# Sums of squares of the attention keys: from column sums and diagonals to a matrix of ones

## What is computed

```python
def mla(c_q, c_kv, k_rope, cq_g, w_uq, ckv_g, w_uk, w_uv, qn_g, kn_g, cos, sin):
    q = (rms_norm(c_q, cq_g) @ w_uq).reshape(b_, t_, MLA_HEADS, QK_HEAD)
    ckv = rms_norm(c_kv, ckv_g)
    k_nope = (ckv @ w_uk).reshape(b_, t_, MLA_HEADS, QK_NOPE)
    v = (ckv @ w_uv).reshape(b_, t_, MLA_HEADS, V_HEAD)
    k_r = jnp.broadcast_to(k_rope[:, :, None, :], (b_, t_, MLA_HEADS, QK_ROPE))
    k = jnp.concatenate([k_nope, k_r], axis=-1)
    q = rms_norm(q, qn_g)
    k = rms_norm(k, kn_g)
    ...
    o = causal_block_attention(q, k, v)
```

## Time and profile before

| | us |
|---|---|
| median of three runs | 1754.62 |
| lowest and highest | 1753.00 and 1754.93 |
| the profiled execution | 1751.97 |
| its span, first to last instruction | 1750.2 |
| PE busy in it | 1734.3 (99%) |
| DVE, ACT, POOL busy | 813.8, 467.3, 1183.7 |
| mean granted TensorE clock | 0.999 of 2.4 GHz |

### The profile page before, as it was taken

The page is one execution under the profiler, slowest core; times in us unless marked ns, Lnnn a source line. Parts: engine busy times, 40 slices in busy tenths (PEclk is TensorE's granted clock), DMA queues, the critical chain, the costliest instruction groups (busy, mean ns, idle before and its releaser), DMA issues.

```text
span 1750.2 us, 32871 instructions
## 1 busy us (share of the span) xinstructions
PE 1734.3 (99%) x12264; PEld 1626.1 (93%) x12264; DVE 813.8 (46%) x1373; ACT 467.3 (27%) x843; POOL 1183.7 (68%) x1365
## 2 busy tenths in 40 slices
PE   7999999999999999999999999999999999999999
PEld 7999999999999999999999999989998888888887
DVE  7755546455555452212347546464555554422221
ACT  4423223242323331101134232332323233311110
POOL 7754746374798777777766647473847988777773
PEclk9999999999999999999999999999999999999999
DMA  4321212122322223222431312222222222422233
GB/s 158 123 96 54 90 59 84 65 74 70 109 84 84 84 96 130 88 96 85 161 112 64 105 56 74 72 84 68 72 77 104 85 93 86 145 88 92 96 121 110
DMA packets 47489, 161.60 MB, mean 92 GB/s; under 512 B 5408, under 2 KB 6816, under 8 KB 47136
## 3 DMA queue, kind: packets, MB, share of 16 engines
q1 hardware_dynamic: 41328, 146.56, 24.6%
q10 hardware_dynamic: 6112, 14.39, 2.2%
HBM read 152.27 MB, written 10.81 MB: 93 GB/s over the span
## 4 chain that ended last, share of the span: by engine, by line
PE 96%; DVE 2%; ACT 1%; issue 0%; ACTq 0%; DVEq 0%
PE slots L508 83%; PE slots L566 4%; PE slots L599 3%; PE slots L542 2%; PE slots L660 2%; PE slots L584 1%; PE slots L551 1%; DVE h_lo L1099 1%; DVE branch_lo L1111 1%; DVE h_tile L1175 0%; PE slots L701 0%; DVE spare L1120 0%; PE slots L569 0%; ACT cq_hi L849 0%; DVE early L1165 0%
## 5 line engine op out<-in xcount | busy, mean ns | idle before, releaser
L420 POOL TENSOR_TENSOR w_lo<-w_raw,w_hi 128x256 fp32r<-128x256 f32 x1004 | 828.4, 855 | 20.9
L415 POOL TENSOR_SCALAR w_hi<-w_raw 128x1024 fp32r<-128x1024 f32 x251 | 284.0, 1131 | 388.1 <-PE slots L508 380.7
L508 PE MATMUL slots<-h_hi,w_hi 128*128 128x264 f32 (+1 forms) x2112 | 522.8, 311 | 0.6
L508 PE MATMUL slots<-h_lo,w_hi 128*128 128x264 f32 (+1 forms) x2112 | 515.9, 308 | 0.0
L508 PE MATMUL slots<-h_hi,w_lo 128*128 128x264 f32 (+1 forms) x2112 | 515.1, 308 | 0.0
L508 PEld LDWEIGHTS slots<-h_hi,w_hi 128*128 128x128 f32 x2112 | 342.7, 188 | 22.9 <-issue 3.9
L508 PEld LDWEIGHTS slots<-h_hi,w_lo 128*128 128x128 f32 x2112 | 342.0, 188 | 19.1
L508 PEld LDWEIGHTS slots<-h_lo,w_hi 128*128 128x128 f32 x2112 | 342.0, 188 | 17.6
L508 PE MATMUL slots<-branch_hi,w_hi 128*128 128x264 f32 (+1 forms) x576 | 144.0, 313 | 9.6 <-DVE branch_lo L1111 8.9
L508 PE MATMUL slots<-branch_lo,w_hi 128*128 128x264 f32 (+1 forms) x576 | 142.8, 311 | 0.0
L508 PE MATMUL slots<-branch_hi,w_lo 128*128 128x264 f32 (+1 forms) x576 | 142.4, 311 | 0.0
(11 more groups left out here) (243 smaller groups left out, 2825.0 us busy)
## 6 DMA issues: line engine op xcount, KB each, us to landing
w_raw<-w_units SPq DMA_DIRECT2D x251, 512.0 KB, 3.2
stream<-sc_acc ACTq DMA_DIRECT2D x16, 264.0 KB, 3.0
sc_back<-stream SPq DMA_DIRECT2D x2, 2112.0 KB, 8.7
x_old<-stream SPq DMA_DIRECT2D x16, 264.0 KB, 4.4
stream<-residual_or_merged ACTq DMA_DIRECT2D x16, 264.0 KB, 2.5
ab_raw<-w_units SPq DMA_DIRECT2D x8, 512.0 KB, 4.6
residual_or_merged<-xt ACTq DMA_DIRECT2D x4, 528.0 KB, 7.6
stream<-xt ACTq DMA_DIRECT2D x1, 2112.0 KB, 10.3
```

The source lines that it names most:

```text
L415: pool.tensor_scalar(hi, raw, 1.0, 1.0, ALU.mult, ALU.mult).then_inc(sem("hi_part"), 1)
L420: op = pool.tensor_tensor(lo[:, cols], raw[:, cols], hi[:, cols].bitcast(F32), ALU.subtract)
L508: mm = pe.matmul(out[:, a_, 0:t1 - t0], w(k), x(k)[:, t0:t1], start=(n == 0), stop=(n == 3 * ks - 1))
```

## The change

The keys' sums of squares are made on all partitions at once. The new `spread_sum` multiplies a 128x128 matrix of ones (the weights) by the squares (what moves, 264 columns at a time), so that PSUM holds the sum for every token on every partition. DVE adds the rope share, which now is a 128x528 tile `kr_sum` in SBUF, ACT takes the root of 528 columns in place, DVE the reciprocal of 528 columns in place, and keys and rope part are multiplied by that tile, which lies in SBUF (`early4`, `early5`). Column sums, diagonals and spreading matmuls for the keys are gone. For kr, `stat_kr` becomes `sum_kr`, copied to SBUF by DVE and multiplied twice by the spread norm of the input.

Several things move with it. The two sums stand between `vb` and `qn0` on PE. `rot` stands behind four pieces of fill; one piece, `stat_q` and nine pieces follow (before: `rot`, two pieces, `stat_q`, twelve pieces; three of them stand inside `stat_q` in both). Of the slots, `qn0` goes to 2, `qn1` to 3, `qr` to 0, `rot` to 2, `stat_q` to 3, and the fills with `av0` and `av1` exchange 0 and 1. In CQ, kr comes before q1, and `rot` behind `stat_q`; DVE's work on q1 stands behind the last column tile of the input's norm.

```diff
-FILLS = (2, 12, 5, 5, 6, 6, 7, 2, 6, 6, 7, 7, 6)
+FILLS = (4, 1, 9, 5, 5, 6, 6, 7, 2, 6, 6, 7, 7, 6)
-           ("stat_kr", 2, "cq_mm"), ("rot", 3, "cq_mm"), ("stat_q", 1, "cq_mm")],
+           ("sum_kr", 2, "cq_mm"), ("stat_q", 1, "cq_mm"), ("rot", 3, "cq_mm")],
-            ("qn0", 0, "att_mm"), ("stat_k", 1, "att_mm"), ("qn1", 2, "unit_used"), ("qr", 3, "att_mm"),
-            ("spread_k0", 0, "att_mm"), ("spread_k1", 1, "att_mm"), ("rot", 3, "att_mm"), ("stat_q", 2, "att_mm"),
...
-            ("g1", 0, "unit_used"), ("b1", 1, "unit_used"), ("ga1", 0, "unit_used"), ("av1", 1, "att_mm")],
+            ("sum_k0", 0, "att_mm"), ("sum_k1", 1, "att_mm"), ("qn0", 2, "att_mm"), ("qn1", 3, "unit_used"),
+            ("qr", 0, "att_mm"), ("rot", 2, "att_mm"), ("stat_q", 3, "att_mm"),
...
+            ("g1", 1, "unit_used"), ("b1", 0, "unit_used"), ("ga1", 1, "unit_used"), ("av1", 0, "att_mm")],
...
+            def spread_sum(out, squares):
+                for a_ in range(2):
+                    mm = pe.matmul(out[:, a_, 0:HALF], ones[0:squares.shape[0], :],
+                                   squares[:, a_ * HALF:(a_ + 1) * HALF], start=True, stop=True)
+                return mm
...
+                    for h in range(2):
+                        out = free("ATT", l, p, f"sum_k{h}")
+                        pe.wait_ge(*at("k_squared", l, p, h + 1))
+                        spread_sum(out, ct[h]).then_inc(sem("att_mm"), 1)
...
-                    act.activation(k_ms[:], k_ms[:], ACT.Sqrt, bias=eps[0:TOK], scale=1.0 / QK)...
+                    for h in range(2):
+                        act.wait_ge(*was_read("ATT", l, p, f"sum_k{h}"))
+                        act.activation(ct[4 + h][:], ct[4 + h][:], ACT.Sqrt, bias=eps, scale=1.0 / QK)...
...
+                dve.tensor_copy(halves(kr_sum), slot(slot_of("CQ", "sum_kr")))...
+                dve.tensor_tensor(halves(kr_sum), halves(kr_sum), slot(slot_of("NORM", "spread")), ALU.mult)...
+                dve.tensor_tensor(halves(kr_sum), halves(kr_sum), slot(slot_of("NORM", "spread")), ALU.mult)...
...
+                    for h in range(2):
+                        dve.tensor_tensor(halves(ct[4 + h][:]), slot(slot_of("ATT", f"sum_k{h}")), halves(kr_sum),
+                                          ALU.add).then_inc(freed("ATT", f"sum_k{h}"), 1)
...
-                        diagonal(ct[4 + h], k_inv, h, "k_diag")
                     for g in range(2):
+                        dve.wait_ge(*at("k_rms", l, p, g + 1))
+                        dve.reciprocal(ct[4 + g][:], ct[4 + g][:]).then_inc(sem("k_rinv"), 1)
...
-                        dve.tensor_tensor(halves(ct[2 + h][:]), halves(ct[2 + h][:]), spread, ALU.mult)...
-                        dve.tensor_tensor(halves(spare[1][rows]), halves(kr_full[rows]), spread[rows], ALU.mult)...
+                        dve.tensor_tensor(ct[2 + h][:], ct[2 + h][:], ct[4 + h][:], ALU.mult)...
+                        dve.tensor_tensor(spare[1][rows], kr_full[rows], ct[4 + h][rows], ALU.mult)...
```

More of the change, by code:

```diff
@@ L281, in build @@
         rope_cos, rope_sin, kr_full, kr_sq = (xm[:, n, :] for n in range(4))
-        probs = xm[:, 4, :]
+        probs, kr_sum = xm[:, 4, :], xm[:, 5, :]
         xg_hi, xg_lo = y_hi, y_lo
@@ L630, in _ @@
                 latent("q2", 5)
-                out = free("CQ", l, 0, "stat_kr")
-                token_sums(out, [kr_sq[0:ROPE]]).then_inc(sem("cq_mm"), 1)
+                out = free("CQ", l, 0, "sum_kr")
+                spread_sum(out, kr_sq[0:ROPE]).then_inc(sem("cq_mm"), 1)
+                out = free("CQ", l, 0, "stat_q")
+                pe.wait_ge(*at("q_lat_summed", l, 0, 2))
+                token_sums(out, [q_lat_sq[0]]).then_inc(sem("cq_mm"), 1)
                 out = free("CQ", l, 0, "rot")
@@ L641, in _ @@
                 mm.then_inc(sem("cq_mm"), 1)
-                out = free("CQ", l, 0, "stat_q")
-                pe.wait_ge(*at("q_lat_summed", l, 0, 2))
-                token_sums(out, [q_lat_sq[0]]).then_inc(sem("cq_mm"), 1)
                 with nc.Fori(0, PAIRS, engines=bass.OrderedEngineSet([pe.engine]), head_slot={pe.engine: 0}) as p:
@@ L692, in _ @@
                             tiles(cq_hi), tiles(cq_lo), KQ).then_inc(sem("att_mm"), 1)
-                    for h in range(2):
-                        out = free("ATT", l, p, f"spread_k{h}")
-                        spread(out, ct[4 + h], lambda t: at("k_diag", l, p, h * NTOK + t + 1)).then_inc(sem("att_mm"), 1)
-                    out = free("ATT", l, p, "rot")
-                    pe.wait_ge(*was_read("ATT", l, p, "qr"))
-                    for a_ in range(2):
-                        mm = pe.matmul(out[:, a_, 0:HALF], rotate, ct[7][:, a_ * HALF:(a_ + 1) * HALF],
-                                       start=True, stop=True)
-                    mm.then_inc(sem("att_mm"), 1)
                     filled = [0]
@@ L721, in _ @@
                     fill(FILLS[0])
+                    out = free("ATT", l, p, "rot")
+                    pe.wait_ge(*was_read("ATT", l, p, "qr"))
+                    for a_ in range(2):
+                        mm = pe.matmul(out[:, a_, 0:HALF], rotate, ct[7][:, a_ * HALF:(a_ + 1) * HALF],
+                                       start=True, stop=True)
+                    mm.then_inc(sem("att_mm"), 1)
+                    fill(FILLS[1])
                     stat = free("ATT", l, p, "stat_q")
@@ L728, in _ @@
                         fill(1)
-                    fill(FILLS[1])
+                    fill(FILLS[2])
                     pe.wait_ge(*at("k_lo", l, p, 2))
@@ L737, in _ @@
                         scores(l, p, n // 5, n % 5)
-                        fill(FILLS[n + 2])
+                        fill(FILLS[n + 3])
                         if n == 5:
@@ L741, in _ @@
                         turn(l, p, n // 5, n % 5)
-                    fill(FILLS[12])
+                    fill(FILLS[13])
                     attend(l, p, 1)
@@ L861, in _ @@
                     h_upper(k)
-                q_latent(1)
+                if l > 0:
+                    act.wait_ge(sem("stored"), l * (16 * KT))
+                act.wait_ge(*ready("CQ", l, 0, "kr"))
+                act.activation(halves(kr_gained[:]), slot(slot_of("CQ", "kr")), ACT.Identity, bias=zero,
+                               scale=hparam(l, KR_G)).then_inc(sem("kr_gained"), 1)
+                act.activation(halves(kr_sq), slot(slot_of("CQ", "kr")), ACT.Square).then_inc(freed("CQ", "kr"), 1)
                 act.wait_ge(*at("kv_ms", l, 0, 1))
@@ L1213, in _ @@
                 dve.tensor_tensor(halves(gatt[1]), halves(kr_gained[:]), slot(slot_of("NORM", "spread")),
[L1214 removed]
+                                  ALU.mult).then_inc(sem("kr_normed"), 1)
                 for n in range(KV):
@@ L1602 @@
         kr = w_in[:, K_ROPE:K_ROPE + ROPE]
-        units += [cols(w_in, C_KV, n) for n in range(KV)] + [cols(w_in, C_Q, n) for n in range(KQ - 1)]
-        units += [cols(np.concatenate([kr, kr], 1), 0, 0), cols(w_in, C_Q, KQ - 1)]
+        units += [cols(w_in, C_KV, n) for n in range(KV)] + [cols(w_in, C_Q, 0)]
+        units += [cols(np.concatenate([kr, kr], 1), 0, 0)] + [cols(w_in, C_Q, n) for n in range(1, KQ)]
         for p in range(PAIRS):
```

112 lines of the change are left out of this document (42 added, 70 removed), and 6 rows, old and new, of tables (SIGNALS, TILES).

## The result

| | before | after |
|---|---|---|
| median of four runs each, side by side, us | 1754.6 | 1767.5 |
| ratio, 95% interval | | 1.0077 (1.0059 to 1.0094) |
| profiled execution, and its span | 1751.97, 1750.2 | 1767.44, 1765.6 |
| PE busy | 1734.3 | 1728.3 |
| mean granted TensorE clock | 0.999 | 0.992 |

The change makes the kernel slower by some 13 us, where 10 less were forecast. The time lies outside the range of 1737 to 1757.

What follows compares the result with a forecast made beforehand. TensorE was taken as the bound, busy 1734.3 of 1750.2 us. Pairs -13.2, slot change +2.0 and latents +0.8 gave -10.4, so 1741.5 for the profiled execution and 1744.2 as median; range 1737 to 1757.

Steps and rivals of the forecast that it cites:

- PE's saving, 2.26 us a pair: TensorE in each attention pair: column sums, spreading matmuls and a wait go, two sums come; 18.1 us in eight pairs.
- The rotation's wait: TensorE's wait on VectorE at the rotation inside a pair, 0.2 us, expected to go behind four fill pieces.
- the last rival: Waits elsewhere on TensorE, for instance at the rotation; half a microsecond a pair would give 1748 to 1750; chance 0.08.
- VectorE's end ahead of the scores: VectorE through qr_lo at 184.4 to 184.9, TensorE there at 184.15; 0.6 us wait taken, 1.65 kept a pair.
- The start (163.1): Time in the second pair of layer 0 when VectorE's first wide reciprocal starts, after ScalarE's root.
- the four products: VectorE's products per pair with the second factor in SBUF: 1.05 us each, 4.2 together, 2.4 to 5.0 possible.
- my bounding rows: Profile rows bounding an SBUF product's price: 0.61 us with a PSUM operand, 0.89 to 1.26 from SBUF alone.
- The reciprocal: VectorE's reciprocal of 528 columns, two a pair: 3.0 us taken, from slopes of 4.2 to 5.8 ns a column.
- slow reciprocal: Rival: wide reciprocals stall TensorE ahead of each pair's first scores; no change at 3.65 us, slower past it; chance 0.14.
- The rival had the price right: Clock rival: 0.6 us waits bring a clock fall at each pair, 1.6 us each, giving 1757; chance 0.07.
- CQ: Stage of the latents, once a layer: moved rotation loses 0.65 to 0.9 us in layer 1, +0.1 in layer 0.
- RG's first tile: x0, sharing slot 0 with av1, must wait for VectorE's read after each layer's last pair: 1.0 us, twice.

## Why the prediction was wrong

- *PE's saving, 2.26 us a pair.* Right in size, in part by luck: 2.47 when nothing waits, 2.1 in the kernel after (PE ready for the scores at 184.28 on the old clock, forecast 184.15). The two new sums took 1.71 us, not 1.89. The rotation's wait, which I took as gone, grew from 1.6 to 2.4 us in eight pairs: VectorE's gain on qr is late there too, the place that the last rival names. The two errors nearly cancel.
- *VectorE's end ahead of the scores.* **The step that failed.** Forecast 184.4 to 184.9, measured 191.56 - 5.43 = 186.1. The start (163.1) was exact. Of 1.7 us too much, the reciprocals at 3.37 from start to start gave 0.74, the four products 0.82 (5.02, the upper bound, where I took the middle, 4.2), the cosine product and the sum 0.67, the two qn_lo took 0.4 back. The stall measured 1.97, and the pairs kept nothing. By my own sum a stall of 1.9 us meant no change, and 1.97 half a microsecond lost. The 15 us between that and the measured span are, from the table, the falls of the clock behind the scores (6.3) and in the first pair (1.6), CQ and the start-up (4.3 over what I had), 2.3 since the pairs kept nothing where 2.26 less 1.97 would have left 0.29 each, and 0.5 that is not placed.
- *Why the products' term was wrong.* Both of my bounding rows were of one kind: operations that happened to run beside GpSimd's work. I read 0.61 against 0.89 to 1.26 as "PSUM or SBUF operand"; the runs show that it takes both, two operands in SBUF and a GpSimd that reads it: with GpSimd idle the same product took 0.62. The first two of the four new products meet GpSimd's sums of squares and its rounding, the next its subtractions, and the cosine product and the sum behind, whose price I took over, got dearer too.
- *The reciprocal.* 3.45 us, against 3.0 and a break-even of 3.65. The slope of the short rows, at 5.8 ns, held for 528 columns within 8% (6.2 ns from 8 to 528 columns: 3448 less 198 over 520). The 5 us that I worked out from the Trainium skill's repeat count of 8 ("VectorE: DVE Perf Modes", First, the fixed hardware budget) don't hold: it took 5.6 times as long as a plain product (0.62 us), not 8 times. The rival "slow reciprocal" named the place and the sign, but not the cause: the end was slower at a reciprocal below its own break-even.
- *The clock.* I held a stall of 0.6 us harmless, and stalls of 1.3 and less were, in 16 pairs and more. At 1.97 four of eight pairs lost 1.6 us each behind the scores. The rival had the price right, but its condition, a fall at 0.6 us, never came up: the stall was three times that. My sum had no term for a longer one. What tells the four pairs from the other four isn't settled.
- *CQ.* Forecast +0.8 for both layers, measured +2.4 and +1.4. I followed the order of the matmuls, and not the slot of the one moved: its slot is freed by VectorE's new products. I had put their cost at nothing, 0.5 at most. That costs 1.55 and 1.62 us, and in layer 0 a fall of the clock that lasts into the first pair (+1.6). The waits at the latents' sums, which I put at about 2 and 1.2 us, were 0.84 in each layer.
- *RG's first tile.* +2.0 forecast, 1.9 measured; the exchange of slots took it away.
- *Start-up.* 1.4 us of the difference of the two profiles belong to no part of the change.

## What to carry to other kernels

An engine that takes over work from the bound one has to be through by the time at which the bound one arrives: write down that time, the busy chain up to it, and the second chain from the last input that comes off the bound engine; if the cover is short, give the bound engine other work there before counting the gain (three pieces turned +13 us into -7). Price a VectorE operation with two SBUF operands by what GpSimd does at that moment, and take both prices, beside it and without it. When a matmul moves, look up who reads the last tile of its slot and which tile is next in it.
